# Hand-over from output projection to feed-forward by token block: the last four and the first four weight tiles multiplied for 128 tokens at a time

## The reference: what is computed

```python
x = x + g1 * y                                   # y = merged @ w_out
h2 = modulate(rmsnorm(x, norm2_g[l]), sh2, sc2)  # rows of 2048 are normed
x = x + g2 * sq_relu_mlp(h2, w1[l], w2[l])       # relu(h2 @ w1)**2 @ w2
```

## Time and profile before

| | |
|---|---|
| median of 3 runs | 1578.26 us |
| lowest, highest | 1577.74, 1579.47 us |
| span of the profiled execution | 1576.3 us |
| TensorE busy | 1516.4 us (96%) |
| VectorE busy | 927.7 us (59%) |
| ScalarE busy | 671.7 us (43%) |
| DMA, HBM read | 354.68 MB, mean 226 GB/s |

### The profile page before, as it was taken

The page is one execution under the profiler, slowest core; times in us unless marked ns, Lnnn a source line. Parts: engine busy times, 40 slices in busy tenths (PEclk is TensorE's granted clock), DMA queues, the critical chain, the costliest instruction groups (busy, mean ns, idle before and its releaser), DMA issues.

```text
span 1576.3 us, 19377 instructions
## 1 busy us (share of the span) xinstructions
PE 1516.4 (96%) x7009; PEld 1206.8 (77%) x7009; DVE 927.7 (59%) x1042; ACT 671.7 (43%) x931; POOL 25.4 (2%) x38
## 2 busy tenths in 40 slices
PE   4989999999999999999998999999999999999996
PEld 1446888878788887877876888888888888888885
DVE  1336665777676668776877554444445455555456
ACT  2324243645544444333345434444434444444443
POOL 0000100101000000000000000000000000000001
PEclk8999999999999999999999999999999999999998
DMA  9999587776676668968883666556555555555551
GB/s 339 321 333 323 198 308 230 257 251 204 203 239 216 210 230 323 315 230 314 319 296 111 195 195 190 183 183 185 167 190 178 207 193 192 194 190 196 189 200 77
DMA packets 108234, 357.61 MB, mean 227 GB/s; under 512 B 11024, under 2 KB 12048, under 8 KB 107024
## 3 DMA queue, kind: packets, MB, share of 16 engines
q1 hardware_dynamic: 105984, 351.32, 65.2%
q10 hardware_dynamic: 2192, 5.51, 0.9%
HBM read 354.68 MB, written 2.10 MB: 226 GB/s over the span
## 4 chain that ended last, share of the span: by engine, by line
PE 87%; DMA 5%; DVE 4%; ACT 2%; issue 1%; POOL 1%; ACTq 0%; SPq 0%; DVEq 0%; POOLq 0%
PE bank L1211 26%; PE bank L1213 26%; PE bank L1212 26%; DMA raw<-in_w_ada 3%; PE bank L1348 2%; PE bank L1330 2%; PE bank L1374 1%; PE bank L1450 1%; DVE wl L909 1%; PE bank L1338 1%; ACT wh L585 1%; DMA raw<-in_w_out 1%; PE bank L1243 1%; DMA raw<-in_w_fourier 1%; DVE acc L929 1%
## 5 line engine op out<-in xcount | busy, mean ns | idle before, releaser
L909 DVE TENSOR_TENSOR wl<-raw,wh 128x1024 fp32r<-128x1024 f32 x464 | 564.0, 1224 | 505.8 <-ACT wh L585 504.8
L585 ACT ACTIVATE wh<-raw 128x1024 fp32r<-128x1024 f32 x464 | 486.1, 1059 | 461.9 <-PE bank L1213 441.4
L1211 PE MATMUL bank<-wh,hT 128*128 128x512 f32 x512 | 209.1, 408 | 3.6 <-DVE wl L909 1.7
L1211 PE MATMUL bank<-wh,h2T 128*128 128x512 f32 x512 | 202.8, 396 | 2.4 <-DVE h2T L1097 2.4
L1213 PE MATMUL bank<-wh,hT 128*128 128x512 f32 x512 | 201.0, 393 | 0.0
L1212 PE MATMUL bank<-wl,hT 128*128 128x512 f32 x512 | 200.2, 391 | 0.0
L1213 PE MATMUL bank<-wh,h2T 128*128 128x512 f32 x512 | 200.0, 391 | 0.0
L1212 PE MATMUL bank<-wl,h2T 128*128 128x512 f32 x512 | 199.6, 390 | 0.0
L1211 PE MATMUL bank<-wh,hidS 128*128 128x512 f32 x512 | 199.5, 390 | 0.0
L1213 PE MATMUL bank<-wh,hidS 128*128 128x512 f32 x512 | 199.4, 390 | 0.0
L1212 PE MATMUL bank<-wl,hidS 128*128 128x512 f32 x512 | 199.4, 389 | 0.0
(11 more groups left out here) (168 smaller groups left out, 1498.9 us busy)
## 6 DMA issues: line engine op xcount, KB each, us to landing
raw<-in_w SPq DMA_DIRECT2D x256, 512.0 KB, 3.6
raw<-in_w_ada SPq DMA_DIRECT2D x192, 512.0 KB, 5.6
raw<-in_w_in SPq DMA_DIRECT2D x128, 512.0 KB, 4.6
raw<-in_w_attn_o SPq DMA_DIRECT2D x32, 512.0 KB, 5.6
raw<-in_w_out SPq DMA_DIRECT2D x32, 512.0 KB, 6.0
raw<-in_w_fourier SPq DMA_DIRECT2D x16, 512.0 KB, 6.0
xt<-in_x ACTq DMA_DIRECT2D x2, 1024.0 KB, 8.6
ct<-in_ctx ACTq DMA_DIRECT2D x2, 1024.0 KB, 14.1
```

The lines of the kernel that those rows point to most:

```text
L585: nc.scalar.activation(slot, raw[:, s % RAW, :], ACT.Copy).then_inc(wh_done, 1)
L909: nc.vector.tensor_tensor(lo, raw[:, s % RAW, :], hi.bitcast(F32), ALU.subtract)\
L1211: nc.tensor.matmul(bank[b][:], a_hi, w_hi, start=first, stop=False)
```

## The change

The last four tiles of `O1` are no longer multiplied bank after bank: for each of them TensorE first does bank 0 alone, when all four are split it does bank 2 for all four, and then banks 1 and 3 tile by tile (`held_products`). Token block 0 is then complete while the products of block 1 are still to be done. The slots of these four tiles are released only in that last part.

The transposes are regrouped: a group is now four feature tiles for one token block, in the order `XS` (block 0 and block 1 in turn). One group stands ahead of the first product instead of three, between the second and third gate matmul. The first four tiles of `w1` are multiplied first for block 0, then for block 1 (`row_product`), with transposes in between; later groups stand behind tiles 4, 5, 8 and 9 (`XS_AFTER`). Step 6 of a group becomes four instructions of 128 columns on ScalarE, and four of 128 and one of 512 on VectorE. On ScalarE and VectorE the order of the residual, squares, splits, scaling and modulation is written out anew, and the later groups stand behind the splits of tiles 3, 4, 6, 7, 9 and 10 (`XS_SPLIT`). `row_squares`, `residual`, `normed` and `gate_2` are the old statements as functions. No matmul, transpose or split is added or dropped.

```diff
-XS_NOW = 3
+HELD = 4
+XS = [(t, g) for g in range(4) for t in range(2)]
+XS_AFTER = {4: (0, 2), 5: (1, 2), 8: (0, 3), 9: (1, 3)}
+XS_SPLIT = {3: (0, 1), 4: (1, 1), 6: (0, 2), 7: (1, 2), 9: (0, 3), 10: (1, 3)}
...
-MISC += GATE2 + [("xs", g) for g in range(8)]
+MISC += GATE2[:2] + [("xs", XS[0])] + GATE2[2:] + [("xs", tg) for tg in XS[1:]]
...
-            for k in range(KT):
+            row_squares(1, 0, ROWS_FIRST[0])
+            row_squares(1, 1, ROWS_FIRST[1])
+            hi_1(0, 0)
+            hi_1(0, 1)
+            gate_2(GATE2[0])
+            gate_2(GATE2[1])
+            row_squares(1, 2, ROWS_FIRST[2])
+            modulate2_hi(XS[0])
+            row_squares(1, 3, ROWS_FIRST[3])
+            gate_2(GATE2[2])
+            gate_2(GATE2[3])
+            hi_1(0, 2)
+            modulate2_hi(XS[1])
+            for k in range(3, KT):
                 hi_1(0, k)
-                if k < AHEAD:
-                    post(M1 - AHEAD + k)
-                if k == AHEAD - 1:
-                    for g in range(XS_NOW):
-                        modulate2_hi(g)
-                if AHEAD <= k and XS_NOW + k - AHEAD < 8:
-                    modulate2_hi(XS_NOW + k - AHEAD)
+                if k in XS_SPLIT:
+                    modulate2_hi(XS_SPLIT[k])
...
+                for j in range(4):
+                    f = 4 * g + j
+                    ins = nc.vector.tensor_scalar(hmod2[:, n % 2, j, :], b[:, j * P:(j + 1) * P], gain2[:, f:f + 1],
+                                                  mods2[:, 0, f:f + 1], ALU.mult, ALU.add)
+                then(ins)
+                nc.vector.tensor_tensor(h2T[1][:, 4 * g:4 * g + 4, t * P:(t + 1) * P], hmod2[:, n % 2, :, :],
+                                        h2T[0][:, 4 * g:4 * g + 4, t * P:(t + 1) * P].bitcast(F32), ALU.subtract)\
+                    .then_inc(misc_free[MISC_AT["xs", tg][0]], 1)
...
-            for k in range(KT):
+            residual(1, 0, ROWS_FIRST[0])
+            residual(1, 1, ROWS_FIRST[1])
+            lo_1(0, 0)
+            lo_1(0, 1)
+            normed(0)
+            residual(1, 2, ROWS_FIRST[2])
+            residual(1, 3, ROWS_FIRST[3])
+            dve.wait_ge(g_done, 2)
+            modulate2_lo(XS[0])
+            normed(1)
+            lo_1(0, 2)
+            modulate2_lo(XS[1])
+            for k in range(3, KT):
                 lo_1(0, k)
...
+                if k in XS_SPLIT:
+                    modulate2_lo(XS_SPLIT[k])
...
+            def held_products(m):
+                def held(b, mm):
+                    k, w, cols_t = TILES[mm][1], slice(b // 2 * HC, (b // 2 + 1) * HC), slice(b % 2 * P, (b % 2 + 1) * P)
+                    return products(b, [(mT[0][:, k, cols_t], mT[1][:, k, cols_t], wh[:, mm % SPL, w], wl[:, mm % SPL, w])],
+                                    False, mm == M1 - 1)
+                ins = held(0, m)
+                if m == M1 - 1:
+                    ins.then_inc(bank_full, 1)
+                    for mm in range(M1 - HELD, M1):
+                        ins = held(2, mm)
+                    ins.then_inc(bank_full, 1)
+                    for mm in range(M1 - HELD, M1):
+                        ins = held(1, mm)
+                        if mm == M1 - 1:
+                            ins.then_inc(bank_full, 1)
+                        held(3, mm).then_inc(gemm_done, 1)
...
+            def xs_transposes(tg):
+                t, g = tg
+                pe.wait_ge(xs_ready, 2 * t + 1 + g // 2)
+                b, full = misc_take(("xs", tg))
+                for j in range(4):
+                    ins = nc.tensor.transpose(b[:, j * P:(j + 1) * P], xs[:, t, (4 * g + j) * P:(4 * g + j + 1) * P], ident[:])
+                ins.then_inc(full, 1)
...
+            pe.wait_ge(mac_step, KT * 8)
+            gate_2(GATE2[0])
+            gate_2(GATE2[1])
+            xs_transposes(XS[0])
+            gate_2(GATE2[2])
+            gate_2(GATE2[3])
+            def row_product(k, t):
+                for b in (t, 2 + t):
+                    if k == 0 and b < 2:
+                        pe.wait_ge(bank_free, 4 * CI1 - 2 * (1 - t))
+                    w = slice(b // 2 * HC, (b // 2 + 1) * HC)
+                    ins = products(b, [(h2T[0][:, k, t * P:(t + 1) * P], h2T[1][:, k, t * P:(t + 1) * P],
+                                        wh[:, k % SPL, w], wl[:, k % SPL, w])], k == 0, False)
+                if t:
+                    ins.then_inc(gemm_done, 1)
...
-            for k in range(KT):
+            misc_wait_freed(pe, ("xs", (0, 0)))
+            for k in range(4):
+                pe.wait_ge(wl_done, W1 + k + 1)
+                row_product(k, 0)
+                if k == 1:
+                    xs_transposes(XS[1])
+            xs_transposes(XS[2])
+            misc_wait_freed(pe, ("xs", (1, 0)))
+            for k in range(4):
+                row_product(k, 1)
+                if k == 1:
+                    xs_transposes(XS[3])
+            for k in range(4, KT):
                 first_product(0, k)
-                if XS_NOW + k < 8:
-                    xs_transposes(XS_NOW + k)
+                if k in XS_AFTER:
+                    xs_transposes(XS_AFTER[k])
```

## The result

The changed kernel takes 1588.43 us (1583.26 to 1590.11, 5 runs), beside 1577.74 us (1577.18 to 1579.47, 5 runs) for the kernel before on the same chip: ratio 1.0063, 95% interval 1.0046 to 1.0079. It is slower by about 10 us. The profiled execution took 1588.43 us, its span is 1586.2 us, 9.9 more than before.

What follows compares the result with a forecast made beforehand. TensorE was taken to bound the kernel, with 87% of the chain. Stops of 14.2 us against 5.23 made it 9.0 slower: span 1576.3 + 9.0 = 1585.3, plus 1.96 outside the span, 1587.2 us; range 1582.5 to 1592.5.

Steps and rivals of the forecast that it cites:

- The bound: Whole kernel: TensorE has 87% of the chain, so only its stops count; those around the hand-over total 5.23 us.
- All six stops: Hand-over: TensorE waits at held tiles 0.79, first product 4.00, tile 3 4.00, tile 4 1.50, tile 10 2.15, tile 11 1.75.
- the tile 3 stop: Block 0's fourth product: its split queues behind the modulation of block 1's first group, stopping TensorE 4.00 us.
- the stops of tiles 10 and 11: Late tiles: splits wait behind a group, at tile 11 also the gate row; 2.15 and 1.75 us.
- The stops of the first product and of tile 4: First product waits 4.00 us for block 0's modulation and splits; tile 4 waits 1.50 us for VectorE's split.
- The narrow group: Four 128-column instructions per group: 1.49 us on ScalarE; 2.15 on VectorE with step wait and subtraction.
- The rival that they cost what wide ones do: Modulation on ScalarE and VectorE: 128-column instructions cost as much as 256-column ones, 1593.3 us; chance 0.08.
- From VectorE's end to TensorE's start: At each hand-over from VectorE: TensorE starts 0.25 us after VectorE ends.
- the held tiles: Projection's end: TensorE reaches tile M1-1 in bank 0 before its low half is ready and stops 0.79 us.
- GpSimd's chain: Between squares and scaling: GpSimd takes 2.29 us until VectorE's scaling, 1.9 for block 1.
- The rival to which I gave 0.22: Granted clock falls in a 4.0 us stop, costing up to 2.4 us: 1589.6 for one, 1592.0 for two; chance 0.22.
- The sum: Whole kernel: stops of 14.2 us against 5.23, 9.0 us slower, 1587.2 us at full clock.

Runs made afterwards that it cites:

- e1: The changed kernel with the split of tile 3 put ahead of the modulation of block 1's first group on ScalarE and VectorE: 1582.43 us, ratio 1.0029 to the kernel before.
- e8: The changed kernel with only the last two groups modulated one split later and the gate row added behind tiles 13 and 14: 1583.77 us, ratio 1.0038.
- e2: The changed kernel with tile 3's split ahead of the modulation, the last two groups one split later and the gate row later: 1578.33 us, ratio 1.0003.
- e6: The changed kernel's parts in an order worked out from measured durations, with a fourth PSUM bank for gates and transposes: 1572.70 us, ratio 0.9970 to the kernel before.
- e11: The kernel before, run once more unchanged: 1577.79 us, ratio 1.0003.
- e3: The changed kernel with three useless matmuls before the first product and three before the fourth product of block 0: 1583.96 us, ratio 1.0038 to the kernel before.
- e7: The kernel before with only the held projection ending and the first two residual pieces and squares ahead of the splits of tiles 0 and 1: 1577.30 us, ratio 0.9997.

## Why the prediction was right, and where its sizes were off

**The bound.** Right. Behind the seam nothing moved: the windows from 912 us on are full at clock 1.00.

**Places and releasers.** All six stops are where the layout put them, and the moves in the two orders of ScalarE and VectorE remove them one at a time: the tile 3 stop by e1, the stops of tiles 10 and 11 by e8, both by e2. The stops of the first product and of tile 4 were not removed singly.

**The narrow group.** ScalarE's four take 1.48 to 1.50 us (1.49 predicted); VectorE's four and the subtraction 1.37 + 0.04 + 0.69 = 2.10 (2.15). The rival that they cost what wide ones do is out. Four narrow ones take VectorE 1.37 us where two wide ones took 1.12; so the rule of the Trainium skill (VectorE: DVE Perf Modes, "The TRN2 errata") that each instruction has a fixed cost points the right way.

**From VectorE's end to TensorE's start** I took 0.25 us from one place. It is 0.05 to 0.06 at five of the six stops (855.54 to 855.59; the first product's `h2T` ends at 845.56) and 0.15 at tile 4. This takes 0.2 off the stops of the first product and of tiles 3 and 10, 0.1 off that of tile 4, and with the narrow group it brings the path from transposes to a usable split to 5.53 us (850.06 to 855.59) instead of 5.83. At the held tiles it is made up for by the matmul behind the stop, which takes 0.34 us. GpSimd's chain is shorter too, here with the row of VectorE's splits of tiles 0 and 1:

```profile
835.26 0.19 POOL L560 TENSOR_TENSOR ss<-ss 128x2 f32<-128x2 f32 x1 [444.62 <-ACT junk L766]
...
836.10 0.58 POOL L535 TENSOR_TENSOR rs<-msum,half_neg 128x1 f32<-128x1 f32 x1
836.16 2.36 DVE L924 TENSOR_TENSOR wl<-raw,wh 128x1024 fp32r<-128x1024 f32 x2 [1.74 <-ACT wh L588]
```

It takes 1.42 us where 2.29 to the scaling were counted, but VectorE was in the splits of tiles 0 and 1 until 838.5 and could not use it; its place in the queue decided. The stops come to 12.85 us where I had 14.2.

**The clock.** The rival to which I gave 0.22 came true, twice in each of the two executions; the forecast had put this term at nothing. I had seen that my stops of 4.0 lay between the 2.42 and 2.55 that "kept it at 1.00" and the 5.12 near the start, and chose the side of the short ones. That step was wrong, twice over. One execution was read as a rule: in the second a stop of 2.43 did not keep the clock. And the stop of 5.12 us, from 15.22 to 20.34, was read only near its end. An earlier window of it is

```profile
16.00:18.00 2.00, 0.00 (x0) 0.93 1.01 411
```

where the clock has already fallen, some 2.5 us into the stop. All ten stops of 3.3 to 4.0 us (idle as shown) in the six profiles that have them let it fall. The size, up to 2.4 us for a fall, was 1.7 in the changed kernel, 2.93 in e1.

**The sum.** The time, 1588.43 for 1587.2 forecast, agrees better than its terms do, and that is luck: stops 1.35 too high, the clock 3.42 too low, the start of the seam 1.3 earlier, and 0.2 more of time outside the span than assumed (2.2 for 1.96). With the kernel's own seam the loss is 11.15 us against one execution of before and 9.4 to 9.6 against the other (83.40 or 83.64 less 74.05), beside 9.0 forecast and 10 measured in the ratio.

What is open: how often the clock falls in the kernel before. Two executions, one with a fall, don't say. It leaves some 1.6 us open in each comparison of one seam with it, and the starts of the seam some 2 us more in a single run. The clock may have a part in their wandering too: adding up one minus the granted clock over windows of 4 us from 0 to 824 us gives 11.9 us for the earliest start (e6, 823.55) and 17.1 for one of the latest (e11, 828.79). But the very latest (e3, 829.36) has 13.6, so it is at most a part, and how much was not worked out.

## What to carry to other kernels

A finer hand-over helps only if each item in each queue stands behind nothing that is due later: here the halves came early enough, and then waited behind a modulation whose input did not exist yet. So lay the queues out in time with measured durations before choosing an order; the same work in another order, with one more bank, went from 0.6% slower to 0.2 to 0.3% faster. And where TensorE must stand for some microseconds, count the slower restart as part of the stop; useless matmuls in the stop can be cheaper than none.

## What had not been expected of the hardware

- A kernel with six more matmuls, none of them of use, ran 0.25% faster than the same without (1.0038 to 1.0063), with a seam 3.1 us shorter.
- The same stops of 2.55 and 2.43 us left the granted clock at 1.00 in one execution and let it fall in another. A stop of 2.32 us in e7 let it fall too. Stops of 3.3 us and more at the hand-over (idle as shown) let it fall in every profile that has them; after stops of up to 1.84 us in the seam no fall was seen.
- A fall does not cost the same each time. Counted as in the changed kernel, ten of the twelve in the seams cost 1.5 to 1.75 us, the one in e1 2.93, and the one in e7, which hit only transposes, 1.3.
- VectorE's result reached a waiting TensorE in 0.05 us at five stops of the changed kernel, in 0.15 at the sixth and in 0.25 at the first product of the kernel before; why these differ was not tried.
